# Second layer of a streaming encoder: the query norm's root in two halves of three tiles, the first made and spread during the projection

## What is computed

```python
def fox_layer(x, kb, vb, cb, km, vm, p, is_prompt):
    x = macaron_half(x, p['g_ffn1'], p['w_ffn1_in'], p['w_ffn1_out'])
    hn = rms_norm(x, p['g_attn'])
    qb, qm = jnp.split(hn @ p['w_in'], [SELF_WIDTH], axis=-1)
    qb = rms_norm(qb.reshape(B, S, H_B, HEAD_DIM), p['g_q'])
    qm = rms_norm(qm.reshape(B, S, H_MEM, HEAD_DIM), p['g_qm'])
    ...
    s = jnp.einsum('bqhd,bkhd->bhqk', qblk, kb).astype(jnp.float32) * SCALE
    decay = jnp.moveaxis(cqblk, 2, 1)[..., :, None] - ck
    pm = jax.nn.softmax(jnp.where(visible, s + decay, NEG_INF), axis=-1)
    ...
    om = memory_attn(qm, km, vm)
    x = x + mix @ p['w_out']
```

## Time and profile before

| | us |
|---|---|
| median of 3 runs | 1273.26 (1273.0 to 1273.76) |
| profiled execution, its own time | 1272.96 |
| its span, first to last instruction | 1271.1 |
| TensorE busy | 1260.7 (99%) |
| VectorE busy | 752.2 (59%) |
| ScalarE busy | 561.7 (44%) |
| GpSimd busy | 188.1 (15%) |
| TensorE's granted clock, mean | 1.000 of full speed |

### The profile page before, as it was taken

How to read it: one execution, slowest core, us unless ns; L and a number is a source line. 1 busy time by engine, 2 the same in 40 slices (tenths; PEclk the granted TensorE clock), 3 DMA queues, 4 the chain that set the end, 5 groups by cost and what they waited for, 6 DMA issues and landing times.

```text
span 1271.1 us, 22398 instructions
## 1 busy us (share of the span) xinstructions
PE 1260.7 (99%) x8772; PEld 1241.2 (98%) x8772; DVE 752.2 (59%) x1133; ACT 561.7 (44%) x829; POOL 188.1 (15%) x208
## 2 busy tenths in 40 slices
PE   9999999999999999999999999999999999999999
PEld 9999999999998999999999999999997899999999
DVE  7766575555676656564555775554456756656433
ACT  6543453343375533433343443333355764343322
POOL 0120021146144000000122000001134410000000
PEclk9999999999999999999999999999999999999999
DMA  8364445643204443444443534354441134343343
GB/s 307 137 177 139 162 150 166 215 166 134 99 34 135 160 160 137 163 168 141 151 167 122 197 133 157 140 165 161 158 167 35 68 133 166 135 162 134 135 140 129
DMA packets 38829, 187.64 MB, mean 148 GB/s; under 512 B 4432, under 2 KB 13008, under 8 KB 23664
## 3 DMA queue, kind: packets, MB, share of 16 engines
q1 hardware_dynamic: 37296, 183.43, 41.7%
q0 software_dynamic: 1184, 3.13, 1.2%
q10 hardware_dynamic: 288, 0.24, 0.1%
HBM read 179.89 MB, written 6.90 MB: 147 GB/s over the span
## 4 chain that ended last, share of the span: by engine, by line
PE 95%; DVE 2%; ACT 1%; issue 1%; DMA 0%; POOL 0%; SPq 0%; DVEq 0%; ACTq 0%
PE bank L503 29%; PE bank L504 29%; PE bank L505 29%; PE bank L779 1%; PE bank L740 1%; PE bank L782 1%; PE bank L749 1%; PE bank L917 1%; DMA x<-in_xT 0%; ACT ew L1316 0%; PE outs L529 0%; POOL mixlo L2212 0%; PE outs L531 0%; PE bank L551 0%; DVE wlo L1557 0%
## 5 line engine op out<-in xcount | busy, mean ns | idle before, releaser
L503 PE MATMUL bank<-xhi,whi 128*128 128x320 f32 (+1 forms) x1760 | 545.8, 310 | 0.6 <-DVE wlo L1938 0.6
L505 PE MATMUL bank<-xhi,wlo 128*128 128x320 f32 (+1 forms) x1760 | 543.0, 309 | 0.0
L504 PE MATMUL bank<-xlo,whi 128*128 128x320 f32 (+1 forms) x1760 | 542.9, 308 | 0.0
L1557 DVE TENSOR_TENSOR wlo<-raw,whi 128x2048 fp32r<-128x2048 f32 (+1 forms) x176 | 361.7, 2055 | 236.3 <-ACT whi L1152 236.1
L1152 ACT ACTIVATE whi<-raw 128x2048 fp32r<-128x2048 f32 (+1 forms) x177 | 304.5, 1720 | 324.5 <-PE bank L505 324.2
L503 PEld LDWEIGHTS bank<-xhi,whi 128*128 128x128 f32 x1760 | 330.6, 188 | 3.2 <-issue 1.5
L504 PEld LDWEIGHTS bank<-xlo,whi 128*128 128x128 f32 x1760 | 330.6, 188 | 0.5
L505 PEld LDWEIGHTS bank<-xhi,wlo 128*128 128x128 f32 x1760 | 330.5, 188 | 0.0
L503 PE MATMUL bank<-hhi,whi 128*128 128x320 f32 x704 | 217.8, 309 | 0.0
L505 PE MATMUL bank<-hhi,wlo 128*128 128x320 f32 x704 | 217.5, 309 | 0.0
L504 PE MATMUL bank<-hlo,whi 128*128 128x320 f32 x704 | 217.5, 309 | 0.0
(11 more groups left out here) (235 smaller groups left out, 1051.7 us busy)
## 6 DMA issues: line engine op xcount, KB each, us to landing
raw<-in_w_ffn_in SPq DMA_DIRECT2D x85, 1024.0 KB, 4.8
raw<-in_w_ffn_out SPq DMA_DIRECT2D x64, 704.0 KB, 4.1
raw<-in_w_in_a SPq DMA_DIRECT2D x10, 1024.0 KB, 4.8
raw<-in_w_out SPq DMA_DIRECT2D x8, 1024.0 KB, 4.7
raw<-in_w_kv SPq DMA_DIRECT2D x6, 1024.0 KB, 4.8
raw<-in_w_mkv SPq DMA_DIRECT2D x4, 1024.0 KB, 4.7
raw<-in_w_in_b SPq DMA_DIRECT2D x4, 1024.0 KB, 4.7
raw<-in_w_ffn_in SPq DMA_DIRECT2D x6, 256.0 KB, 6.5
```

The costliest lines, as they stand in the source:

```text
L503: mm(acc, wh, mhi(ks[q]), start=start and q == 0, stop=False)
L504: mm(acc, wh, mlo(ks[q]), start=False, stop=False)
L505: last = mm(acc, wl, mhi(ks[q]), start=False, stop=stop and q == nk - 1)
L1557: tt(wlo[slot][:, 0:size], raw[slot][:, 0:size], f32(whi[slot][:, 0:size]), ALU.subtract).then_inc(lo_ready[slot], 1)
```

## The change

The group `pb_q` is cut into `pb_q` (query tiles 0 to 2) and a new `pb_r` (tiles 3 to 5), each with a root of its own. The statistics of `pb_q` lag one tile instead of two. Its root is made by ScalarE and VectorE at tile 5 of the projection, and its three spreads use the two spare banks: two behind tile 6, the third inside tile 7. VectorE scales the three query tiles there. The statistics of `pb_r` are begun behind tile 7 and finished in the attention, and its root stands later in the attention than the old one did, on ScalarE before the exponentials of unit 3. The query rows 0 to 2 and their waits leave the attention, and the scores of unit 3 go ahead of the values of unit 1.

```diff
-         "sub": (5, 6, 18), "kv": (6, 6, 24), "pb_m": (7, 2, 30), "pb_q": (8, 6, 32)}
+         "sub": (5, 6, 18), "kv": (6, 6, 24), "pb_m": (7, 2, 30), "pb_q": (8, 3, 32), "pb_r": (9, 3, 35)}
...
+AUX0["pb_q"] = AUX0["pb_m"] + 2
...
TensorE:
                 def query_row(j):
 
-                    pe.wait_ge(hr_ready, HNORM["pb_q"][0] + 1)
-                    if j:
-                        pe.wait_ge(hs_free, j)
-                    mm(HS[:, 0:R], pair_of(j), rs[:, 0:R], start=True, stop=True).then_inc(hs_ready, 1)
+                    pe.wait_ge(hr_ready, HNORM["pb_r"][0] + 1)
+                    if j > 3:
+                        pe.wait_ge(hs_free, j - 3)
+                    mm(HS[:, 0:R], pair_of(j - 3), rs[:, 0:R], start=True, stop=True).then_inc(hs_ready, 1)
...
-                    head_stat("pb_q", 4, R)
-                    head_stat("pb_q", 5, R)
+                    head_stat("pb_r", 1, R)
+                    head_stat("pb_r", 2, R)
                     values(0)
                     scores(2)
                     turns_of(1)
-                    query_row(0)
+                    scores(3)
                     values(1)
-                    pe.wait_ge(hs_free, 1)
-                    query_row(1)
-                    scores(3)
-                    pe.wait_ge(hs_free, 2)
-                    query_row(2)
                     scores(4)
                     turns_of(2)
                     values(2)
...
-                      [AUX0["pb_m"] + 2] * 9]
+                      [AUX0["pb_q"] + 3] * 9]
...
                 if j == 5:
                     head_broadcast("pb_m", AUX0["pb_m"], R)
-
-            projection("pb", R, [("pb_m", 0, 2), ("pb_q", 2, 2)], 8, after=after_pb, before=before_pb)
+                if j == 6:
+                    head_broadcast("pb_q", AUX0["pb_q"], R, [0, 1])
+
+            def within_pb(k):
+                if k == 4:
+                    head_broadcast("pb_q", AUX0["pb_q"] + 2, R, [2])
+
+            projection("pb", R, [("pb_m", 0, 2), ("pb_q", 2, 1), ("pb_r", 5, 2)], 8, after=after_pb, before=before_pb,
+                       within=within_pb)
...
ScalarE:
                     exps(1, 0)
                     exps(1, 1)
-                    head_root("pb_q", R)
                     copy_first(1)
                     copy_rest(1)
                     out_hi(0)
...
                     out_copy(1)
                     out_hi(1)
+                    head_root("pb_r", R)
                     exps(3, 0)
                     exps(3, 1)
                     copy_first(2)
...
-            projection("pb", R, [("pb_m", 0), ("pb_q", 2)], 8, tile_b, {3: "pb_m"}, True,
+            projection("pb", R, [("pb_m", 0), ("pb_q", 2), ("pb_r", 5)], 8, tile_b, {3: "pb_m", 5: "pb_q"}, True,
...
VectorE:
                     invert(1, 1, True)
-                    head_root("pb_q", R)
-                    queries(0)
                     maxima(2, 0)
                     maxima(2, 1)
-                    queries(1)
                     maxima(3, 0)
                     invert_both(2)
                     maxima(3, 1)
-                    queries(2)
+                    head_root("pb_r", R)
                     invert_both(3)
...
                 if j == 6:
+                    for q in range(2):
+                        query_row(q)
                     maxima_b()
 
-            projection("pb", R, 8, tile_b, {3: "pb_m"}, True, after_pb,
-                       before=lambda j: inverse_b() if j == 7 else None)
+            def query_row(q):
+                dve.wait_ge(aux_ready, AUX0["pb_q"] + q + 1)
+                query_scale(q, "qb", aux[(AUX0["pb_q"] + q) % 2], aux_free)
+
+            def before_pb(j):
+                if j == 7:
+                    inverse_b()
+                    query_row(2)
+
+            projection("pb", R, 8, tile_b, {3: "pb_m", 5: "pb_q"}, True, after_pb, before=before_pb)
```

More of the change, by code:

```diff
@@ L74 @@
 HNORM = {"mkv0": (0, 2, 0), "mkv1": (1, 2, 2), "pa_k": (2, 6, 4), "pa_q": (3, 6, 10), "pa_m": (4, 2, 16),
-         "sub": (5, 6, 18), "kv": (6, 6, 24), "pb_m": (7, 2, 30), "pb_q": (8, 6, 32)}
+         "sub": (5, 6, 18), "kv": (6, 6, 24), "pb_m": (7, 2, 30), "pb_q": (8, 3, 32), "pb_r": (9, 3, 35)}
 IN_MS = ("pa_q", "pb_m")
-HEAD_FREE = {"mkv0": 0, "mkv1": 1, "pa_k": 2, "pa_q": 2, "pa_m": 3, "sub": 5, "kv": 6, "pb_m": 7, "pb_q": 7}
+HEAD_FREE = {"mkv0": 0, "mkv1": 1, "pa_k": 2, "pa_q": 2, "pa_m": 3, "sub": 5, "kv": 6, "pb_m": 7, "pb_q": 7, "pb_r": 9}
 AUX0 = {"mkv0": 0}
@@ L897, in run_memory_first @@
                         turns_of(i)
-                        pe.wait_ge(hs_free, min(i, 6))
+                        if i > 3:
+                            pe.wait_ge(hs_free, min(i, 6) - 3)
                         if i < 6:
@@ L1886, in queries @@
                     def queries(q):
-                        dve.wait_ge(hs_ready, q + 1)
+                        dve.wait_ge(hs_ready, q - 2)
                         query_scale(q, "qb", HS, hs_free)
@@ L2237, in run_memory_first @@
                         if i == 0:
-                            head_squares_lo("pb_q", lambda j: qk[:, j, :], R, acc_free,
-                                            lambda j: TILE0["pb"] + 2 + j + 1, [5])
+                            head_squares_lo("pb_r", lambda j: qk[:, 3 + j, :], R, acc_free,
+                                            lambda j: TILE0["pb"] + 5 + j + 1, [2])
                         if i >= 2:
@@ L2284, in _ @@
             head_squares_lo("pb_m", lambda j: qk[:, 6 + j, :], R, acc_free, lambda j: TILE0["pb"] + j + 1)
-            head_squares_lo("pb_q", lambda j: qk[:, j, :], R, acc_free, lambda j: TILE0["pb"] + 2 + j + 1, range(5))
+            head_squares_lo("pb_q", lambda j: qk[:, j, :], R, acc_free, lambda j: TILE0["pb"] + 2 + j + 1)
+            head_squares_lo("pb_r", lambda j: qk[:, 3 + j, :], R, acc_free, lambda j: TILE0["pb"] + 5 + j + 1, range(2))
             attention(1)()
```

## The result

| | before | after |
|---|---|---|
| median of 20 runs each | 1273.11 (1272.43 to 1275.71) | 1276.13 (1275.21 to 1278.16) |
| profiled execution | 1272.96 | 1276.96 |
| its span | 1271.1 | 1275.1 |
| its granted clock, mean | 1.000 | 1.000 |

Forecast were 2.1, and 1276.13 is inside the range.

A forecast was written before the change was run, and what follows sets the result against it. The prediction took TensorE to bound the kernel, busy 1260.7 of 1271.1 us. It added 2.1 us to the profiled 1272.96 for 1275.1, then 0.3 for the runs' median: 1275.4 us, range 1273.4 to 1276.9.

The forecast's parts named there:

- Step 1: Projection, before tile 5: statistics one tile earlier make TensorE wait for GpSimd's low squares, 1.1 us.
- Step 2: Projection, behind tile 6: TensorE waits for the first root before two spreads, 0.6 us.
- Step 3: Three spreads moved ahead of the attention, 0.45 us; with both new waits, unit 1's first scores come 2.15 us late.
- Step 4: Attention up to unit 2's turning: the 1.30 us wait and 0.86 us of query rows go, all 2.15 is back.
- Step 5: Attention: ScalarE's second root, 1.8 us, delays values 2 from 984.03 to 985.7 and unit 4's exponentials by 2.2 us.
- Step 6: Attention's remainder: neither TensorE nor ScalarE can make up the delay, so 2.1 us stay at the end.
- slower, TensorE's clock: Rival, chance 0.08: the 2.9 us stop before values 2 halves TensorE's clock, costing 2.1 us more, total 1277.5.
- slower by over 0.2%: Whole-kernel outcome above 1275.8 us, given a chance of 0.28.
- within 0.2%: Whole-kernel outcome of a time within 0.2% of before, given a chance of 0.68.

The follow-up runs named there:

- e5_lock: Changed kernel with VectorE's subtraction of the low weights made to wait for GpSimd's low squares of query tile 3; 1277.95 us, one execution, against 1273.18 before.
- e2_root: Changed kernel with the second root back near the old root's place on ScalarE and VectorE; 1273.74 us, 1.0002 of before.
- e7_filler: Changed kernel with seven useless matmuls on TensorE between the turning and the values of unit 2; 1275.25 us, 1.0017 of before.
- e6_longstop: Changed kernel with eight useless ScalarE copies between the second root and the exponentials of unit 3; 1277.67 us, 1.0039 of before.
- e3_both: Changed kernel with the edits of e1_stats and e2_root, the three early spreads left in place; 1272.82 us, 0.9995 of before.
- e4_all: Changed kernel with the edits of e1_stats and e2_root, and all three early spreads inside tile 7; 1272.67 us, 0.9993 of before.
- e8_best: e4_all with query statistic 2 moved from behind tile 5 into tile 6, behind the memory tiles' spread; 1271.89 us, 0.999 of before.
- e8_again: The kernel of e8_best measured once more in another set; 1272.01 us, 0.999 of before.
- e1_stats: Changed kernel with its first three query statistics placed one behind tile 4 and two behind tile 5; 1275.23 us, 1.0015 of before.

## Why the prediction was right, and by how much not

Starts of after are given in before's clock, that is less 1.99.

- *Step 1, the low squares.* Tile 5's product starts at 956.07 (forecast: 1.1 late on 954.94, so 956.04). The wait of 0.85 that the view names is only part of it, since the engine's idle time is counted from a modelled end. That the 2.54 us was real and a lock, e5_lock shows.
- *Step 2, the first root.* Its spreads start at 964.21, forecast 964.2.
- *Step 3 and the sum.* The turning of unit 1 is at 975.44, forecast 975.4.
- *Step 4, what comes back.* The turning of unit 2 is at 981.68, forecast 981.7. That the early loss is given back is shown by e2_root, which has all of it and ends 0.27 late.
- *Step 5, ScalarE.* `copy_first(2)` starts at 984.29 (984.5), the values of unit 2 at 985.45 (985.7) behind a stop of 2.63 (2.9), the exponentials of unit 4 at 986.21 (986.3). I had 0.2 too much between the two copies: 7.72 us instead of 7.95. The root was right (982.42 to 984.20, 1.78 of 1.8). What was too long is the 6.16 of old work, which held the full length of two instructions that idle time followed before; now the next instruction starts 0.1 before the end of each.
- *Step 6, no recovery.* The last divisions are 2.04 late, forecast 2.1. e2_root takes 1.78 of it away by the root's place alone, and e7_filler, with the same 55.90 at full clock throughout, shows that the clock has no part in it. e2_root keeps the two new stops of the projection and has no clock loss either, so those stops aren't what lowers it. But "neither engine has room" is too strong: of TensorE's 1.6 us behind the stop of e6_longstop 0.6 was made up.

Two readings were off without harm. The two stops for `pt` of the earlier trace rows don't both stand in the second layer: that of 1.28 is in the first, and only the 1.22 was within reach, which is the figure that the sums use. And the windows of the earlier trace rows leave out 975.7 to 989 us, where the stop of 1.22 lies; the granted clock is 1.00 there as well.

What failed is the weight of a rival, "slower, TensorE's clock". I gave it 0.08 as a case by itself, at 2.1 us. In truth it comes on top of the forecast in some executions and not in others: 22 of 31, about 1.0 us each by the medians. That accounts for the 0.9 by which the change cost more than forecast (3.0 against 2.1), of which 0.7 show in the median (1276.13 against 1275.4), since before came out 0.15 lower. It is why "slower by over 0.2%", at 0.28, came true by the medians and "within 0.2%", at 0.68, didn't, though the interval begins at 0.16%. That the median still lies inside the range is in part luck: no term of the sum stood for the clock.

The price was too high too, 2.1 where the runs show 1.0. I took it from the slow matmuls at the start of the program. The view of before shows a granted clock of 1.00 there, and then the usual distances begin:

```profile
1.30:5.30 4.00, 4.00 (x15) 3.99 (x16) 1.77 (x6) 2.57 (x4) 0.00 (x0) 1.00 0.87 234
```

```profile
5.40 0.31 PE L503 MATMUL bank<-xhi,whi 128*128 128x320 f32 x1
5.55 0.31 PE L504 MATMUL bank<-xlo,whi 128*128 128x320 f32 x1
```

But the trace of before has no record of the clock until 5.38 us, where the first one says full speed, and in the trace of after that record stands at 6.59, again where the distances fall to 0.147. So the 1.00 ahead of it is the absence of a record. These matmuls are 0.287 apart, nearly as the 0.27 at a recorded 0.50 in e5_lock. That they ran at half clock is likely by this, but not shown. Per matmul, then, the price was about right. What was wrong is how many matmuls pay it and that all of it stays: behind the stop of e6_longstop TensorE lost 1.6 us, and the stretch kept 1.0.

The Trainium skill (TensorE: Matmul & The Clock Gate, Why this matters for your kernels) warns of idle gaps between bursts of matmuls. The runs agree that a stop alone does it: with the stop of 2.63 the clock fell in most executions, with 3.89 in all five, and with 1.22 in none of the 54 of e2_root, e3_both, e4_all, e8_best and e8_again; before, with stops of 1.30 and 1.22, shows it in 1 of the 76 executions whose clock is on record.

## What to carry to other kernels

Before an instruction is moved on an engine that isn't the bound, count the unbroken work between the two points at which the bound waits for that engine: 44% busy says nothing of the stretch of 8 us that counts, and four short instructions cost 1.8 us there. A cost can hide behind a gain: the change's 2.04 us are 2.62 lost and 0.58 won, and only taking the places back one by one shows both. A statistic moved one tile forward is late by what the slowest of its producers takes in that very place, here under a neighbour's lock. And a stop that is harmless by its length can cost again through the clock, in some executions only: look at the granted clock of every run, not of the profiled one alone.

## What the runs showed that I had not expected

- A stop of 2.63 us on TensorE lowers the granted clock in about two of three executions (22 of 31, and 8 of 11 of e1_stats), and useless matmuls that fill it keep the clock up in 11 of 11 and save 0.8 to 1.0 us of the median at an unchanged stretch (2.07 over before, against 2.84 and 3.02).
- Two stops of 0.73 and 0.82 us with one matmul between them were followed by half clock in the one execution of e5_lock, where a single stop of 1.22 was in none of the 54 above.
- Eight ScalarE copies of 64 partitions x 40 columns took 1.10 us together, 0.14 each.
- The view's granted clock of 1.00 at the start of a program means nothing until the trace's first record of it, here at 5.38 and 6.59 us.
